# Causal mask of the prompt attention: added by VectorE in PSUM in place of an identity product on TensorE

## The reference

```python
Q_BLOCK = 128
N_HEADS = 16
SM_SCALE = 1.0 / math.sqrt(QK_NOPE + QK_ROPE)      # 64 + 32
...
s = (einsum("bqhc,bkc->bhqk", qlb, ckv) + einsum("bqhr,bkr->bhqk", qpb, kr)) * SM_SCALE
qpos = i * Q_BLOCK + arange(Q_BLOCK)
s = where(kpos[None, :] <= qpos[:, None], s, -1e30)
p = softmax(s, axis=-1)
o = einsum("bhqk,bkc->bqhc", p, ckv)
```

## Time and profile before

| | us |
|---|---|
| median of 3 runs | 4160.64 (4159.44 to 4164.02) |
| the profiled execution, its own time | 4161.57 |
| its span, first to last instruction | 4159.8 |
| prompt attention loop, first scores to first gather of the cache | 2222.97 to 2391.84 |
| of these 168.9 us, the three `project` calls inside, product part alone | 14.00, 14.00, 15.70 |

### The profile page before, as it was taken

How to read it: one execution, slowest core, us unless ns; L and a number is a source line. 1 busy time by engine, 2 the same in 40 slices (tenths; PEclk the granted TensorE clock), 3 DMA queues, 4 the chain that set the end, 5 groups by cost and what they waited for, 6 DMA issues and landing times.

```text
span 4159.8 us, 63189 instructions
## 1 busy us (share of the span) xinstructions
PE 2915.5 (70%) x24987; PEld 1072.8 (26%) x24987; DVE 2418.7 (58%) x5697; ACT 1245.9 (30%) x3808; POOL 1208.7 (29%) x1088
## 2 busy tenths in 40 slices
PE   4455966867766766566679986776867766866666
PEld 3344441402202200000436633341402201300000
DVE  8453129786775776455324432229686776776645
ACT  1311014434333333233212211104434334334333
POOL 6100003444444444233000000003443444444332
PEclk7767986868767767667889987876877767866766
DMA  8664049999999999999101011149999999999998
GB/s 331 159 221 140 20 183 385 399 420 415 409 421 419 410 414 420 406 418 389 64 30 42 16 74 69 56 169 388 383 420 413 404 420 420 409 420 407 417 419 333
DMA packets 208878, 1263.84 MB, mean 304 GB/s; under 512 B 54488, under 2 KB 55392, under 8 KB 62520
## 3 DMA queue, kind: packets, MB, share of 16 engines
q0 software_dynamic: 151552, 1109.46, 65.2%
q1 hardware_dynamic: 56480, 150.09, 10.6%
q10 hardware_dynamic: 576, 0.59, 0.0%
HBM read 1247.58 MB, written 10.12 MB: 302 GB/s over the span
## 4 chain that ended last, share of the span: by engine, by line
DMA 35%; PE 30%; DVE 19%; issue 10%; ACT 5%; SPq 1%; POOL 1%; DVEq 1%; PEldq 0%; POOLq 0%; ACTq 0%
DMA arena<-peer_uv,arena 32%; PE psum L2127 9%; DVE arena L1659 7%; PE psum L2074 6%; PE psum L2043 3%; DVE arena L1313 3%; PE psum L2382 2%; PE psum L2205 1%; DVE arena L1322 1%; PE psum L2178 1%; DVE arena L1570 1%; ACT arena L1138 1%; ACT arena L1135 1%; ACT arena L1123 1%; PE psum L2266 1%
## 5 line engine op out<-in xcount | busy, mean ns | idle before, releaser
L2127 PE MATMUL psum<-arena 32*32 32x512 f32 x16384 | 1591.2, 852 | 807.4 <-ACT arena L1138 792.8
L1659 DVE SCALAR_TENSOR_TENSOR arena<-arena 128x1024 f32<-128x1024 f32 x1040 | 1275.0, 1226 | 786.4 <-DMA arena<-peer_uv,arena 774.7
L920 POOL DMA_INDIRECT arena<-peer_uv,arena x1040 | 1107.8, 1065 | 2141.6 <-PE psum L2127 1526.3
L2127 PEld LDWEIGHTS psum<-arena 32*32 32x32 f32 x16384 | 219.6, 121 | 2067.9 <-ACT arena L1138 2000.8
L1123 ACT ACTIVATE arena<-arena 128x1 f32<-128x1 f32 x1040 | 210.6, 202 | 1570.3 <-DVE arena L1659 1564.6
L1138 ACT ACTIVATE arena<-arena 128x32 f32<-128x32 f32 x1024 | 329.1, 321 | 33.4
L1135 ACT ACTIVATE arena<-arena 128x1 f32<-128x1 f32 x1040 | 306.0, 294 | 33.8
L2074 PE MATMUL psum<-arena 128*128 128x128 f32 x2048 | 269.7, 289 | 7.3 <-DMA arena<-peer_wq 6.2
L2074 PEld LDWEIGHTS psum<-arena 128*128 128x128 f32 x2048 | 251.6, 202 | 80.4 <-issue 78.8
L1313 DVE TENSOR_TENSOR arena<-arena 128x512 f32<-128x512 f32 (+5 forms) x182 | 155.1, 852 | 92.9 <-ACT arena L1229 74.6
L1962 PE MATMUL psum<-arena 128*9 128x128 f32 x2048 | 98.6, 372 | 117.0 <-DMA arena<-b_mod 117.0
(11 more groups left out here) (248 smaller groups left out, 2749.6 us busy)
## 6 DMA issues: line engine op xcount, KB each, us to landing
arena<-w_mod SPq DMA_DIRECT2D x64, 1024.0 KB
arena<-peer_uv,arena POOLq DMA_INDIRECT x1040
arena<-peer_wq SPq DMA_DIRECT2D x8, 2048.0 KB, 16.4
arena<-w_glu SPq DMA_DIRECT2D x4, 2048.0 KB, 12.5
arena<-x_prompt SPq DMA_DIRECT2D x4, 1024.0 KB
arena<-x_after_layer SPq DMA_DIRECT2D x8, 512.0 KB
arena<-w_o SPq DMA_DIRECT2D x1, 4096.0 KB
arena<-mod_rows SPq DMA_DIRECT2D x2, 1536.0 KB
```

The lines of the kernel that those rows point to most:

```text
L920: pool.indirect_dma_start(ring[r], None, a[f"peer_uv{t // 5}"], bass.IndirectOffsetOnAxis(ap=ix, axis=0)).then_inc(landed[r], 16)
L1659: dve.scalar_tensor_tensor(out=u, in0=u, scalar=1.0, in1=h, op0=ALU.mult, op1=ALU.mult, accum_out=at(DOTS + (t % 2) * 2 * P + m, 1)).then_ ...
L2127: ins = pe.matmul(acc_of(t, i, c), diag[rows, r, :], ring[r][rows, D + 512 * c:D + 512 * (c + 1)], start=(m == 0), stop=last, skip_group_c ...
```

## The change

The product with the identity is removed from TensorE's list, and the scores product ends its accumulation group and raises `s_S` itself. VectorE adds the triangle onto the last 128 columns of the bank, in place in PSUM, before it takes the maximum. The add waits for the scores (and, from the third head on, for the exponential of head n_ - 2); the maximum now waits for the add.

```diff
@@ attention_dve, per head
                         nm = stat[:, 32 + n_ % 2:33 + n_ % 2]
                         if n_ >= 2:
                             dve.wait_ge(s_e2, n_ - 1)
+                        tt(psum[:, n_ % 2, P * i:w], psum[:, n_ % 2, P * i:w], at(MASK, P), ALU.add)
                         link(dve.tensor_reduce(nm, psum[:, n_ % 2, 0:w], AX.X, ALU.max))
                         dve.tensor_scalar(nm, nm, -SM_SCALE, None, ALU.mult).then_inc(s_nm, 1)
@@ attention_pe, per head
                         pe.matmul(psum[:, n_ % 2, 0:w], qtm[0:QKD, h, P * i:w], kt_[0:QKD, h, 0:w], start=True,
-                                  stop=False, skip_group_check=True)
-
-                        pe.matmul(psum[:, n_ % 2, P * i:w], ident, at(MASK, P), start=False, stop=True,
-                                  skip_group_check=True).then_inc(s_S, 1)
+                                  stop=True).then_inc(s_S, 1)
```

## The result

The changed kernel takes 4170.75 us in the median of 12 runs (4160.89 to 4178.37), the kernel before 4160.25 in 12 runs beside them (4156.99 to 4168.05). The ratio is 1.0024, with a 95% interval of 1.0014 to 1.0034: it is slower by about 10 us. The forecast was 4163.2, within a range of 4157.5 to 4171.0.

A forecast was written before the change was run, and what follows sets the result against it. The prediction took TensorE as nearly full, with a loop of engine steps over two heads close behind or bounding. Terms summed to +2.5 us, 4164.1 from the profiled time or 4163.1 from the median; forecast 4163.2, range 4157.5 to 4171.

The forecast's parts named there:

- The loop of steps: Attention loop, two heads: scores, mask, maximum, exponential, transpose, value products, next scores; forecast to grow 0.09 us per two heads.
- The slope of 39 us per us of the add: Whole program: each us of add price costs about 39 us, from 32 half-loops plus about seven places in VectorE's queue.
- The whole sum: All terms over tiles, head_scale and projections: 0.7 + 0.7 - 2.3 + 1.4 + 1.2 + 0.8 = +2.5 us.
- the clock falls in the loop: Third rival: tile 0 at 1.2 GHz, +4.4 us (4167.6), 3%; tile 1 too, another 8.8 (4176), 3%.
- tile 1 without masks is as full as tile 0 is now: Argument against the clock falling: TensorE in tile 1 stays as busy as tile 0 before, which had clock 1.00.
- the gaps stay under 0.6 us: Argument against the clock falling: TensorE's gaps in the loop stay below 0.6 us after the change.
- lengthened those waits by 0.4 us each: Behind each of three projections, two adds lie on the path, one offset by the missing mask product: together +1.2 us.
- the dear add: Second rival: VectorE's write to PSUM in all 64 heads is dear; at 0.50 us per add, +10.7 us (4171); 8%.
- TensorE as the bound: First rival: TensorE bounds the loop everywhere, so removing 64 products wins 14.7 us less projection waits, about 4147; 2%.

The follow-up runs named there:

- e7: The changed kernel with filler products of identity and mask on TensorE in its loop waits and at the projections; ratio 0.9998 to the kernel before, loop 171.1 us.
- the filled forms: The changed kernel (e7) and the kernel before (e8), each with filler products on TensorE where it waits; loops 171.1 and 168.0 us.
- the hybrid: Kernel with TensorE's mask product in tiles 0 and 1 and VectorE's add in tiles 2 and 3; ratio 1.0047 unfilled, 0.9990 with gaps filled.
- e8: The kernel before with filler products behind and at the projections and in front of the sample part's cache waits; ratio 0.9979, loop 168.0 us.
- e9: The hybrid with filler products only in the gaps behind and at the projections, none in a head's own wait; ratio 0.9990, loop 169.5 us.
- e11: The changed kernel without its add (neither product nor add), with filler products in tiles 0 and 1 and at the projections; ratio 0.9968, loop 159.5 us.
- e3: The changed kernel without its add, so neither product nor add and no filler; ratio 1.0027 to the kernel before, loop 178.8 us.
- e4: The hybrid without filler, against the kernel before; ratio 1.0047, loop 192.7 us.

## Why the prediction was right in range and wrong in its mechanism

**What held.** The range held the time, by 0.25 us (4170.75, its end was 4171.0), and that is luck: the main term of the loss was not in the sum, and in both pairs of traces a shorter sample part hid some of it. The forecast's own steps held one by one. The add costs 0.298 us (0.29 taken). The loop of steps grows by about 0.1 us per two heads. At 1.00 tile 0 takes 2.17 in e7 (2.15 was forecast), and in the changed kernel itself tile 1 takes 2.96 (2.93), tile 2 3.74 (3.7), tile 3 4.52 (4.44). The slope of 39 us per us of the add gave 12.4, measured 12.5. The whole sum was +2.5; between the filled forms, at equal clock, it is +3.1.

**What failed** is the step "the clock falls in the loop", given 6% in all. It came, in both traces, and it is the larger part of the loss. The loops add up as follows: 183.1 - 171.1 = 12.0 us that the low clock costs the changed kernel, + 3.1 for the change at full clock, - 0.8 for what the kernel before itself loses against its filled form: 14.3, the difference of the two profiles. An estimate of the 12.0 by place: tile 0 about 4.5 (8 pairs, 2.73 in place of 2.17), the first and third projections 4.4 (15.49 and 16.91 in place of 14.00), the heads of tile 1 the rest, about 3. The price of the rival was right (2.70 per two heads in tile 0, measured 2.73), the chance was not.

Two arguments had made it small. One was "tile 1 without masks is as full as tile 0 is now", which looked at the share of work in steady state. For tile 1 that held: its later heads stayed at 1.00 without masks, 12.87 us busy of 14.80. The falls began elsewhere, tile 1's inside the wait of 2.28 us behind the projection and tile 0's in the opening of the loop. The other was "the gaps stay under 0.6 us". That was true of the heads in steady state (one of 0.72 us in mid-tile 1 apart), but not of the opening, where the wait before the first transposes went from 0.62 to 1.17 us. Nor was it true behind the projections: the prediction had itself lengthened those waits by 0.4 us each, as time only, and did not ask what 2.28 us in place of 1.72 does to the clock. That the time came out slower is this rival, not the dear add.

What the runs show, then: with the waits filled, both kernels and the hybrid keep 1.00 through the whole loop (e7, e8, e9), and the changed kernel wins back 12.0 us. What they leave open: no run fills the opening of tile 0 alone or the first wait of tile 1 alone, and the length of one wait doesn't decide it (0.95 us at the opening with and without a fall, 2.00 us behind a projection with and without).

The Trainium skill ("TensorE: Matmul & The Clock Gate", "A second HAM failure mode: psum-queue depth-cycling") describes a kernel that cycles through PSUM banks with small idle gaps between its groups of products and so falls back and forth between the clock's levels. Tile 0 after the change agrees in part: TensorE waits 0.3 to 0.5 us for ScalarE in each pair of heads and the granted clock is 0.56. But it fell once and stayed down, and did not go back and forth. I had let the kernel before decide, whose gaps are smaller.

**What the sum over the program leaves open.** In the two pairs of traces the loop lost 14.3 and 11.3 us, mean 12.8, and the sample part, whose instructions are the same, was 5.9 and 4.4 shorter (349.7 and 350.5, against 355.6 and 354.9). Together +7.6, beside +10.5 in the medians. 1.7 and 1.5 us of the shorter sample part are the last projection's products, 14.00 us in place of 15.70 and 15.54. For the rest I have no cause; variants with the same instructions there had 349.9 to 355.5, and no run tells it apart.

**The other rivals.** TensorE as the bound, with up to 14.7 us to win, is out: even with product and add both gone the loop wins 8.5 us at full clock (e11). A dear write to PSUM is out by the row of the add.

## What to carry to other kernels

Before taking work off TensorE, look at how long its longest gaps become, the one at the start of a loop too, and what the granted clock does in places of the same trace with gaps like these; a product that seems a waste may hold the clock. Add up the stages of two profiles one by one, since here 14 us lost in one stage hid behind 6 us in the next and 7 in the parts that the change doesn't touch. And where a wait can't be removed, products into a bank that is overwritten anyway are a cheap trial: 22 us of 4160 came from them here, without touching the algorithm.

## What was not expected of the hardware

- After a fall the clock can stay at 1.2 GHz while TensorE has no gap at all: 30 us of 30 busy at 0.50 in e3's tile 1, and over 30 us in e4's tile 2, both behind one gap of about 2 us (1.94 and 2.00). In the changed kernel tile 1 came back to 1.00 after 10 us. What makes the difference wasn't tried.
- Doing less made the kernel slower: 64 products fewer and nothing added, +0.27% (e3).
- VectorE's tensor_tensor from PSUM into the same PSUM columns costs 0.298 us at 128x128, about as much as the copy out of PSUM of this width (0.292).
